# The two expert rows of a token are added into its residual row by the gathering DMA itself

## The chip, the cores and the metric

The kernel runs on one core of a Trainium2 chip. The metric is the device time of one execution in microseconds (us); before the change the median of three executions is 1997.67 us (1995.52 to 1998.90).

## The reference, cut to what matters

One layer of a hybrid encoder: a token mixer, an attention over a memory, and a hierarchical mixture of experts, each followed by a DeepNorm residual and a layer norm. The change touches the last of them alone. There are T = 1056 tokens of D = 1024 f32 values, and each token goes to two of 32 experts:

```
x = LN3(alpha * x + y[token, first expert] + y[token, second expert]),   alpha = 2 ** 0.25
LN: xc = x - mean(x);  xc * rsqrt(mean(xc * xc) + 1e-5) * g + b
```

The expert rows y already carry their gate factor.

## The kernel before

It is one program with an instruction stream for each engine, ordered by semaphores. SBUF is one large array, the arena, and its regions are reused from stage to stage. Tokens are handled in NT = 9 tiles of 128 rows (the ninth has 32). The residual rows after the second layer norm stay in SBUF as `x1` (nine tiles of 128x1024 f32) and are also stored to HBM, from where the experts' inputs are gathered.

**The expert loop** runs over 32 experts, then over spilled blocks (an expert takes at most C = 96 rows in its first block; two spilled blocks occur in this run). Per expert SP loads three weight matrices of 2 MB, PE multiplies in gate/up (L785) and down (L794) form, DVE turns blocks and finishes the silu (L1743 to L1756, in `dve_expert`), ACT scales the result by the gate and stores it to `y_blocks` in HBM (L1263, L1268). POOL gathers the inputs of an expert two ahead (L1938), as soon as DVE has turned the input block that used the buffer (L1756).

**The tail** starts when the last expert rows have landed in HBM; ACT then signals `fin_ready` (L1326). POOL issues 18 indirect DMAs (L1967), two for each tile: one into `g1` (the first expert's rows) and one into `g2` (the second's), both on the tile's semaphore `g_in[t]`. For six of the tiles (2, 4, 5, 6, 7, 8) POOL adds the pair itself (`pair_sum`, L1962), two tiles behind its gathers; for tiles 0, 1 and 3 DVE adds it (L1822). DVE then makes `alpha * x1 + g1` (L1825) and signals `sum_ready`. ACT takes the row sums with a copy pass (L1333), the negative mean (L1334, `mean_ready`), the squares (L1336) and the scale (L1337, L1338, `rstd_ready`). DVE centres the tile before (L1830), then scales the one before that (L1837), and SP stores each tile when DVE has scaled it (L880). The DVE loop is a software pipeline: in step s it sums tile s, centres tile s-1 and scales tile s-2, in this order, so the scaling of a tile always stands behind the centring of the next one.

Of the kernel before, what the change touches and what calls it, by code (L numbers as in the profile page):

```python
# [8 lines left out]
ALU = mybir.AluOpType  # L9
# [4 lines left out]
D = 1024  # L14
# [3 lines left out]
NT = (T + P - 1) // P  # L18
# [12 lines left out]
ALPHA = 2.0 ** 0.25  # L31
# [10 lines left out]
def rows_of(t):  # L42
    return P if t < NT - 1 else DEC


def cols_of(t):
    return slice(t * P, t * P + rows_of(t))


def build(nc, io):  # L50
    ctx = ExitStack()
    with ctx:
        def sem(name):
            return ctx.enter_context(nc.semaphore(name))
# [6 lines left out]
        def const(n):  # L61
            a = cpos[0]
            cpos[0] += n
            assert cpos[0] <= NCONST, cpos[0]
            return consts[:, a:a + n]
# [32 lines left out]
        dest_i = const(2 * NT).bitcast(U32).rearrange("p (k t) -> p k t", t=NT)  # L98
# [12 lines left out]
        def at(a, n):  # L111
            assert a + n <= ARENA, (a, n)
            return arena[:, a:a + n]

        def view(_at, names, **n):
            size = 1
            for v in n.values():
                size *= v
            return at(_at, size).rearrange(f"p ({names}) -> p {names}", **n)
# [41 lines left out]
        x1 = view(R, "t n", t=NT, n=D)  # L161
# [60 lines left out]
        place = route("k t n", k=2, t=NT, n=2 * NB)  # L222
        assert rt[0] <= R + 17408
        g1 = view(0, "t n", t=NT, n=D)
        g2 = view(NT * D, "t n", t=NT, n=D)
        scrap = at(R + 9216, D)
        PAIRS_DVE = (0, 1, 3)
        PAIRS_POOL = [t for t in range(NT) if t not in PAIRS_DVE]

        psum = ctx.enter_context(nc.psum_tensor("psum", [P, 8 * BANK], F32))  # L230

# [1 line left out]
        y_dram = nc.dram_tensor("y_blocks", [NB * C, D], F32, kind="Internal").ap()  # L233
# [34 lines left out]
        x2_stored = sem("x2_stored")  # L268
# [10 lines left out]
        o_xt, o_gu, o_h, o_dn, o_y = (sem(n) for n in ("o_xt", "o_gu", "o_h", "o_dn", "o_y"))  # L279
        o_gate = sem("o_gate")  # L280
        g_in = [sem(f"g_in{i}") for i in range(NT)]
        sum_ready, pair_ready = sem("sum_ready"), sem("pair_ready")
        fin_ready, mean_ready, centered = sem("fin_ready"), sem("mean_ready"), sem("centered")

        def banked(ps):
# [30 lines left out]
        def filled(eng, key):  # L316

            n, banks, _, _ = jobs[key]
            eng.wait_ge(pe_done, n)
            return psum[:, banks[0] * BANK:(banks[-1] + 1) * BANK]  # L320
# [6 lines left out]
        def emptied(eng, key):  # L327
            _, _, c, n = jobs[key]
            eng.wait_ge(evac[c], n + 1)
# [10 lines left out]
        def chain_of(eng, s):  # L340
            n = [0]

            def link(ins):
                n[0] += 1
                ins.then_inc(s, 1)
                eng.wait_ge(s, n[0])
            return link
# [49 lines left out]
        def score_cols(i):  # L397
            return (i + 1) * P if i < NT - 1 else PAST + DEC
# [661 lines left out]
        def _(act):  # L1060
            A = nc.scalar.activation
            link = chain_of(act, act_chain)
# [11 lines left out]
            for t in range(NT):  # L1074
                n = rows_of(t)
# [30 lines left out]
            for p, (tiles, nbuf, _, lag) in enumerate(FOX):  # L1106
                steps = [(i, h) for i in tiles for h in range(FH)]
                for s in range(len(steps) + lag + 3):
                    if s < len(steps):
                        i, h = steps[s]  # L1110
                        k = (FOX_FIRST[p] + s) // FH
# [5 lines left out]
                        nq, n = rows_of(i), score_cols(i)  # L1117
# [66 lines left out]
            for s in range(len(HG) + 2):  # L1184
                if s < len(HG):
                    n = rows_of(HG[s][1])
                    copy_job(("KE", s), keT[0:n, s % 3, :], filled(act, ("KE", s))[0:n, 0:P])
                if 0 <= s - 2 < len(HG):
                    h, c = HG[s - 2]
                    n = rows_of(c)  # L1190
# [37 lines left out]
            for s in range(NT + 3):  # L1228
                if s < NT:
                    n = rows_of(s)  # L1230
# [8 lines left out]
                if 1 <= s <= NT:  # L1239
                    u = s - 1  # L1240
                    n = rows_of(u)
# [4 lines left out]
                if s >= 3:  # L1246
                    u = s - 3
                    n = rows_of(u)
# [79 lines left out]
            for t in range(NT):  # L1328
                n = rows_of(t)
                y = x1[0:n, t, :]  # L1330
                total, neg_mean, squares, log_var, scale = (vals[0:n, i, t:t + 1] for i in range(5))
                act.wait_ge(sum_ready, t + 1)
                link(A(scrap[0:n, :], y, ACT.Copy, accum_out=total))  # L1333
                A(neg_mean, total, ACT.Copy, scale=-1.0 / D).then_inc(mean_ready, 1)  # L1334
                act.wait_ge(mean_ready, t + 1)
                link(A(scrap[0:n, :], y, ACT.Square, bias=neg_mean, accum_out=squares))  # L1336
                link(A(log_var, squares, ACT.Ln, bias=eps_ln[0:n, :], scale=1.0 / D))  # L1337
                A(scale, log_var, ACT.Exp, scale=-0.5).then_inc(rstd_ready, 1)  # L1338
# [3 lines left out]
        def _(dve):  # L1342
            V = nc.vector
            link = chain_of(dve, dve_chain)
            TS, TT, STT = V.tensor_scalar, V.tensor_tensor, V.scalar_tensor_tensor
# [4 lines left out]
            for t in range(NT):  # L1350
                n = rows_of(t)
# [41 lines left out]
            for p, (tiles, nbuf, _, lag) in enumerate(FOX):  # L1393
                steps = [(i, h) for i in tiles for h in range(FH)]
                for s in range(len(steps) + lag + 3):
                    if s < len(steps):
                        i, h = steps[s]
                        ps = filled(dve, ("S", p, s))
                        nq, n = rows_of(i), score_cols(i)
# [3 lines left out]
                    if (p, s) in FV_STEPS and FV_STEPS.index((p, s)) % 4 == 3:  # L1403
                        t = FV_LATE[FV_STEPS.index((p, s)) // 4]
                        n = rows_of(t)
# [13 lines left out]
                    if 0 <= u < len(steps) and u % FH == 0:  # L1419
                        i, k = tiles[u // FH], FOX_FIRST[p] // FH + u // FH  # L1420
# [14 lines left out]
            for m in range(HH):  # L1435
                k = hk[:, m, :]
# [4 lines left out]
            for m in range(HH):  # L1441
# [3 lines left out]
                for c in range(NT):  # L1445
                    b = hb[:, m, cols_of(c)]
# [44 lines left out]
            for t in range(NT):  # L1491
                n = rows_of(t)
# [10 lines left out]
            for s in range(len(HG) + 2):  # L1503
                if s < len(HG):
                    h, c = HG[s]
                    n = rows_of(c)
# [120 lines left out]
            for s in range(NT + 4):  # L1627
                if s < NT:
                    n = rows_of(s)
# [7 lines left out]
                if s >= 4:  # L1637
                    u = s - 4
                    n = rows_of(u)
# [8 lines left out]
                if 1 <= s <= NT:  # L1648
                    u = s - 1
                    n = rows_of(u)  # L1650
# [52 lines left out]
            for k, (E, GG) in enumerate(((E1, GA), (E2, GB))):  # L1703
                for t0, t1 in ((0, NT - 1), (NT - 1, NT)):
                    n, nt = rows_of(t0), t1 - t0
# [46 lines left out]
            def turn_h(b):  # L1752
                return V.transpose(hhT[:, b], hh.rearrange("p s (d k) -> p s k d", k=KE))  # L1753
# [4 lines left out]
            def x_turned(e, b, j):  # L1758
                dve.wait_ge(xe_in[b], 16 * NS * j + 16 * NS)
                if not isinstance(e, int) or e > 1:  # L1760
                    dve.wait_ge(gu_done, e - 1)
                turn_x(b).then_inc(xt_ready, 1)

            def dve_expert(e, b, j, last_one=False):

                if not last_one:
                    x_turned(e + 1, 1 - b, j + b)
                dve.wait_ge(g_exp, e + 1)
                silu_up(b, 4 * e)
                if not isinstance(e, int) or e > 1:  # L1770
                    dve.wait_ge(y_done, e - 1)
                turn_h(b).then_inc(h_ready, 1)
                if not isinstance(e, int) or e > 1:
                    dve.wait_ge(y_ready, e - 1)
                V.tensor_copy(gate2[:, b:b + 1, :], gates[:, bass.ds(e, 1), :]).then_inc(gate_ready, 1)

            x_turned(0, 0, 0)
            dve_expert(0, 0, 0)
            dve_expert(1, 1, 0)
            dve_expert(2, 0, 1)  # L1780
            with dve.Fori(1, NE // 2 - 1) as i:
                dve_expert(2 * i + 1, 1, i)
                dve_expert(2 * i + 2, 0, i + 1)
# [29 lines left out]


            dve.wait_ge(ln3_loaded, 32)
            for s in range(NT + 2):
                if s < NT:
                    n = rows_of(s)
                    y, g = x1[0:n, s, :], g1[0:n, s, :]
                    if s in PAIRS_DVE:  # L1820
                        dve.wait_ge(g_in[s], 32)
                        link(TT(g, g, g2[0:n, s, :], ALU.add))  # L1822
                    else:
                        dve.wait_ge(pair_ready, PAIRS_POOL.index(s) + 1)
                    STT(y, y, ALPHA, g, ALU.mult, ALU.add).then_inc(sum_ready, 1)  # L1825
                if 1 <= s <= NT:
                    t = s - 1
                    n = rows_of(t)
                    dve.wait_ge(mean_ready, t + 1)
                    STT(g1[0:n, t, :], x1[0:n, t, :], vals[0:n, 1, t:t + 1], ln3_par[0:n, 0, :], ALU.add, ALU.mult)\  # L1830
                        .then_inc(centered, 1)
                if s >= 2:
                    t = s - 2
                    n = rows_of(t)
                    dve.wait_ge(centered, t + 1)
                    dve.wait_ge(rstd_ready, 2 * NT + t + 1)
                    STT(x1[0:n, t, :], g1[0:n, t, :], vals[0:n, 4, t:t + 1], ln3_par[0:n, 1, :], ALU.mult, ALU.add)\  # L1837
                        .then_inc(ln_ready, 1)
# [3 lines left out]
        def _(pool):  # L1842
            Q = nc.gpsimd
            link = chain_of(pool, pool_chain)
# [79 lines left out]
            for t in range(NT):  # L1924
                n = rows_of(t)
# [30 lines left out]
                    gather(NE + j, j % 2, o_x[j % 2])  # L1956

            pool.wait_ge(fin_ready, 1)
            def pair_sum(t):
                n = rows_of(t)  # L1960
                pool.wait_ge(g_in[t], 32)
                Q.tensor_tensor(g1[0:n, t, :], g1[0:n, t, :], g2[0:n, t, :], ALU.add).then_inc(pair_ready, 1)  # L1962

            for t in range(NT):
                n = rows_of(t)
                for k, g in enumerate((g1, g2)):
                    pool.indirect_dma_start(out=g[0:n, t, :], out_offset=None, in_=y_dram,  # L1967
                                            in_offset=bass.IndirectOffsetOnAxis(ap=dest_i[0:n, k, t:t + 1], axis=0))\
                        .then_inc(g_in[t], 16)
                if t - 2 in PAIRS_POOL:  # L1970
                    pair_sum(t - 2)
            for t in range(NT - 2, NT):
                if t in PAIRS_POOL:
                    pair_sum(t)

# [28 lines left out]
```

## Time and profile before

| | |
|---|---|
| median of three executions | 1997.67 us |
| the profiled execution, its own time | 1996.47 us |
| its span in the trace | 1994.1 us |
| busy: PE, DVE, ACT, POOL | 90%, 38%, 16%, 11% of the span |
| PE's last matmul ends | about 1929 us |
| `fin_ready` given (L1326) | 1935.2 us |
| first and last gather of the tail issued | 1935.4 and 1969.6 us |
| last store issued | 1991.7 us |

The span is the time from the first to the last record of the profiled execution. Its own time lies 2.4 us above the span and 1.2 us under the median. Times below are us from the start of the span unless said otherwise. The tail is the 59 us from 1935 to 1994.

### The profile page before, as it was taken

What the parts mean: (1) busy time and instruction counts of PE and PEld (TensorE: products, weight loads), DVE (VectorE), ACT (ScalarE), POOL (GpSimd) and SP (SyncE); (2) the same over time, 40 slices, a digit from 0 to 9 for tenths busy, and PEclk for the clock granted to TensorE, in tenths of its full rate; (3) what the DMA queues carried; (4) which work ended last, traced back from release to release, by engine and by line L of the source; (5) the groups of instructions that cost most, each with busy time, mean ns of one, the idle gap of its engine ahead of it and who ended that gap; (6) DMA issues with size and microseconds to landing.
All of it is one profiled execution on the core that took longest, in us unless ns stands there. A gap on an engine that the chain in (4) does not pass through costs nothing. (4 is left out here: it accounts for less than half of the span.)

```text
span 1994.1 us, 33667 instructions
## 1 busy us (share of the span) xinstructions
PE 1792.5 (90%) x14867; PEld 1131.6 (57%) x14867; DVE 750.0 (38%) x1089; ACT 309.1 (16%) x701; POOL 210.5 (11%) x196
## 2 busy tenths in 40 slices
PE   8999999999999779999998999939999999999650
PEld 4455568766654554445665665426666666666420
DVE  1111456534461653320012443364433333333227
ACT  1111223411010440111001111000101111111005
POOL 2100000000010420000000000032111111111016
PEclk9999999999999689999999999859999999999875
DMA  5341002001100203045111000349999999999826
GB/s 197 96 165 43 1 5 83 1 1 43 42 0 4 92 6 116 33 136 169 34 42 42 22 22 28 144 171 366 422 424 424 424 425 423 424 424 424 360 61 216
DMA packets 72862, 326.94 MB, mean 164 GB/s; under 512 B 13368, under 2 KB 27968, under 8 KB 59728
## 3 DMA queue, kind: packets, MB, share of 16 engines
q1 hardware_dynamic: 47840, 280.70, 35.1%
q10 hardware_dynamic: 17360, 22.03, 3.4%
q0 software_dynamic: 7584, 23.08, 3.2%
q8 instruction: 61, 1.00, 0.2%
q14 instruction: 17, 0.14, 0.0%
HBM read 288.05 MB, written 37.65 MB: 163 GB/s over the span
## 5 line engine op out<-in xcount | busy, mean ns | idle before, releaser
L785 PE MATMUL psum<-arena 128*32 128x256 f32 x6528 | 360.4, 380 | 32.0 <-issue 30.8
L418 PE MATMUL psum<-arena 128*128 128x352 f32 x1152 | 342.1, 460 | 0.0
L785 PEld LDWEIGHTS psum<-arena 128*32 128x32 f32 x6528 | 244.7, 110 | 146.5 <-issue 45.4
L427 PE MATMUL psum<-arena 128*128 128x512 f32 (+1 forms) x720 | 318.4, 601 | 5.9 <-DMA arena<-in_w_in 4.7
L418 PEld LDWEIGHTS psum<-arena 128*128 128x128 f32 x1152 | 219.3, 191 | 122.2 <-issue 1.1
L1348 DVE COPY arena<-psum 128x512 f32<-128x512 f32 (+7 forms) x135 | 90.9, 681 | 417.8 <-PE psum L427 221.6
L427 PEld LDWEIGHTS psum<-arena 128*128 128x128 f32 (+1 forms) x720 | 131.7, 185 | 177.4 <-issue 175.5
L794 PE MATMUL psum<-arena 128*32 128x256 f32 x3264 | 189.7, 389 | 24.1 <-DVE arena L1753 24.1
L794 PEld LDWEIGHTS psum<-arena 128*32 128x32 f32 x3264 | 125.4, 113 | 82.0 <-DVE arena L1753 25.5
L1743 DVE TENSOR_SCALAR arena<-arena 128x384 f32<-128x384 f32 x34 | 12.2, 360 | 357.1 <-ACT arena L1284 315.3
L1065 ACT ACTIVATE arena<-psum 128x128 f32<-128x128 f32 (+5 forms) x181 | 86.5, 495 | 349.8 <-PE psum L411 276.2
L1938 POOL DMA_INDIRECT arena<-x_rows,consts x102 | 96.7, 948 | 414.1 <-DVE arena L1756 386.0
L411 PE MATMUL psum<-consts,arena 128*128 128x128 f32 (+4 forms) x819 | 121.8, 280 | 12.4 <-ACT arena L1065 6.3
L411 PEld LDWEIGHTS psum<-consts,arena 128*128 128x128 f32 (+4 forms) x819 | 97.2, 154 | 59.0 <-issue 30.8
L643 PE MATMUL psum<-arena 128*128 128x512 f32 (+1 forms) x288 | 125.3, 593 | 0.0
L1545 DVE SCALAR_TENSOR_TENSOR arena<-arena,psum 128x1024 f32<-128x1024 f32 (+1 forms) x18 | 22.0, 1220 | 185.8 <-PE psum L427 103.8
L1263 ACT ACTIVATE arena<-psum,consts 128x256 f32<-128x256 f32 x102 | 40.9, 471 | 324.0 <-DMA y_blocks<-arena 270.6
L643 PEld LDWEIGHTS psum<-arena 128*128 128x128 f32 (+1 forms) x288 | 51.5, 181 | 68.3 <-issue 67.9
L1745 DVE RECIPROCAL arena<-arena 128x384 f32<-128x384 f32 x34 | 86.8, 2553 | 1.2
L546 PE MATMUL psum<-arena 128*128 128x64 f32 (+2 forms) x624 | 76.5, 266 | 0.0
L511 PE MATMUL psum<-arena 66*128 66x512 f32 (+3 forms) x192 | 75.6, 502 | 0.5 <-DVE consts L1348 0.5
L1118 ACT ACTIVATE arena<-psum,consts 128x128 f32<-128x128 f32 (+8 forms) x72 | 51.3, 713 | 150.5 <-DVE consts L1401 148.7
(243 smaller groups left out, 1402.1 us busy)
## 6 DMA issues: line engine op xcount, KB each, us to landing
arena<-in_moe_w_down SPq DMA_DIRECT2D x34, 2048.0 KB, 22.6
arena<-in_moe_w_gate SPq DMA_DIRECT2D x34, 2048.0 KB, 16.9
arena<-in_moe_w_up SPq DMA_DIRECT2D x34, 2048.0 KB, 22.0
arena<-in_w_in SPq DMA_DIRECT2D x7, 2048.0 KB, 9.8
y_blocks<-arena ACTq DMA_DIRECT2D x136, 96.0 KB, 2.0
y_blocks<-arena ACTq DMA_DIRECT2D x1, 8448.0 KB, 44.0
arena<-in_x_prompt SPq DMA_DIRECT2D x9, 512.0 KB, 3.3
arena<-in_w_out SPq DMA_DIRECT2D x2, 2048.0 KB, 11.0
```

What stands on the lines that cost most here:

```text
L411: return nc.tensor.transpose(out, a, ident[0:n, 0:n])
L418: last = mm(ps[0:m, c * BANK:c * BANK + THIRD], lhs(k), rhs[:, k, c * THIRD:(c + 1) * THIRD], start=(k == 0), stop=(k == KD - 1))
L427: last = mm(ps[0:n, c * 512:(c + 1) * 512], lhs(k), rhs(k, c), start=(k == 0), stop=(k == KD - 1))
L511: last = mm(ps[0:nq, c:e], q, ka[0:KX, h, c:e], start=True, stop=True)
L546: last = mm(ps_o[0:nq, h * FD:(h + 1) * FD], probsT[p][0:w_, u % nbuf, b, 0:nq], v, start=(b == 0), stop=(b == len(blocks) - 1))
L643: last = mm(psum[0:n, b:b + BANK], mixT[:, k, cols_of(t)], wrows[:, k, c * 512:(c + 1) * 512], start=(k == 4), stop=(k == 3))
L785: last = mm(out, xeT[:, b, a, k, :], gu[b][:, :, k, j * P:(j + 1) * P], start=(k == 0), stop=(k == KD - 1))
L794: last = mm(B_Y[b][32 * j:32 * j + 32, a * 256:(a + 1) * 256], hhT[:, b, a, k, :], wd[b][:, k, j * 256:(j + 1) * 256], start=(k == 0), sto ...
L1065: take(A(out, src, ACT.Copy), key)
L1348: take(V.tensor_copy(out, src), key)
L1745: V.reciprocal(sg, sg).then_inc(silu_step, 1)
L1938: pool.indirect_dma_start(out=xe[:, b, a, :], out_offset=None, in_=x2_quarters, in_offset=bass.IndirectOffsetOnAxis(ap=tok_idx[:, e, a:a + ...
```

## The change

- The gathers of the tail write `x1` itself with an addition: the DMA adds each gathered row to what stands in SBUF. `g2`, `pair_sum`, DVE's pair sums and DVE's `alpha * x1 + g1` go.
- Two additions into one tile may not be in flight together, so POOL first issues the first rows' gather of tile s, and then waits for the landing of tile s-3's before it issues the second rows' gather of that tile (`GATHER_LAG = 3`).
- `x1` must hold `alpha * x1` before. DVE does this in the expert loop: three tiles each behind experts 0, 1 and 2, once the rows are stored to HBM. POOL waits for all nine (`x2_scaled`).
- ACT's row sums and DVE's centring wait for the gathers' semaphore (32, both landed) where they had waited for DVE or POOL.

```
-            dve_expert(0, 0, 0)
-            dve_expert(1, 1, 0)
-            dve_expert(2, 0, 1)
+            dve.wait_ge(x2_stored, 16 * NT)
+            for e, b, j in ((0, 0, 0), (1, 1, 0), (2, 0, 1)):
+                dve_expert(e, b, j)
+                for t in range(3 * e, 3 * e + 3):
+                    y = x1[0:rows_of(t), t, :]
+                    TS(y, y, ALPHA, None, ALU.mult).then_inc(x2_scaled, 1)
...
-            for s in range(NT + 2):
-                if s < NT:
-                    n = rows_of(s)
-                    y, g = x1[0:n, s, :], g1[0:n, s, :]
-                    if s in PAIRS_DVE:
-                        dve.wait_ge(g_in[s], 32)
-                        link(TT(g, g, g2[0:n, s, :], ALU.add))
-                    else:
-                        dve.wait_ge(pair_ready, PAIRS_POOL.index(s) + 1)
-                    STT(y, y, ALPHA, g, ALU.mult, ALU.add).then_inc(sum_ready, 1)
-                if 1 <= s <= NT:
+            for s in range(1, NT + 2):
+                if s <= NT:
                     t = s - 1
                     n = rows_of(t)
+                    dve.wait_ge(g_in[t], 32)
                     dve.wait_ge(mean_ready, t + 1)
...
-            def pair_sum(t):
-                n = rows_of(t)
-                pool.wait_ge(g_in[t], 32)
-                Q.tensor_tensor(g1[0:n, t, :], g1[0:n, t, :], g2[0:n, t, :], ALU.add).then_inc(pair_ready, 1)
...
+            def add_rows(k, t):
+                n = rows_of(t)
+                pool.indirect_dma_start(out=x1[0:n, t, :], out_offset=None, in_=y_dram,
+                                        in_offset=bass.IndirectOffsetOnAxis(ap=dest_i[0:n, k, t:t + 1], axis=0),
+                                        compute_op=ALU.add).then_inc(g_in[t], 16)
+
+            pool.wait_ge(x2_scaled, NT)
+            for s in range(NT + GATHER_LAG):
+                if s < NT:
+                    add_rows(0, s)
+                if s >= GATHER_LAG:
+                    pool.wait_ge(g_in[s - GATHER_LAG], 16)
+                    add_rows(1, s - GATHER_LAG)
```

## Rows read from the trace of the kernel before

**Rows 1.** The page: busy time of each engine.

```profile
PE 1792.5 (90%) x14867; PEld 1131.6 (57%) x14867; DVE 750.0 (38%) x1089; ACT 309.1 (16%) x701; POOL 210.5 (11%) x196
```

**Rows 2.** Chain that ended last, in order of time (start, us, what).

```profile
1934.95 0.21 ACT consts L1326
...
1935.42 0.94 POOL arena L1967
...
1970.53 2.65 POOL arena L1962
```

**Rows 3.** Groups by line, 1935 to 1995 (busy us, mean ns, idle before).

```profile
L1967 POOL DMA_INDIRECT arena<-y_blocks,consts x18 | 22.6, 1256 | 102.6 <-ACT consts L1326 97.8 <-issue 4.7
L1962 POOL TENSOR_TENSOR arena<-arena 128x1024 f32<-128x1024 f32 (+1 forms) x6 | 15.9, 2668 | 0.1
L1830 DVE SCALAR_TENSOR_TENSOR arena<-arena 128x1024 f32<-128x1024 f32 (+1 forms) x9 | 13.6, 1508 | 0.0
L1837 DVE SCALAR_TENSOR_TENSOR arena<-arena 128x1024 f32<-128x1024 f32 (+1 forms) x9 | 13.5, 1505 | 0.0
L1825 DVE SCALAR_TENSOR_TENSOR arena<-arena 128x1024 f32<-128x1024 f32 (+1 forms) x9 | 13.1, 1456 | 6.8 <-POOL arena L1962 6.7
...
L1822 DVE TENSOR_TENSOR arena<-arena 128x1024 f32<-128x1024 f32 x3 | 3.7, 1221 | 21.2 <-DMA arena<-y_blocks,consts 21.2
```

**Rows 4.** Timeline of the tail (start, duration, engine, line).

```profile
1944.34 1.06 ACT L1333 ACTIVATE arena<-arena 128x1024 f32<-128x1024 f32 x1 [9.18 <-DVE arena L1825]
...
1945.52 0.20 ACT L1334 ACTIVATE arena<-arena 128x1 f32<-128x1 f32 x1
...
1947.70 1.06 ACT L1333 ACTIVATE arena<-arena 128x1024 f32<-128x1024 f32 x1
...
1969.64 0.88 POOL L1967 DMA_INDIRECT arena<-y_blocks,consts  x1 [0.30 <-issue]
...
1976.47 3.38 DVE L1830 SCALAR_TENSOR_TENSOR arena<-arena 128x1024 f32<-128x1024 f32 x1
...
1989.22 2.46 DVE L1837 SCALAR_TENSOR_TENSOR arena<-arena 128x1024 f32<-128x1024 f32 x2
1991.71 0.33 SPq L880 DMA_DIRECT2D out_y_s<-arena  x1
```

**Rows 5.** DMA, 1936 to 1976: queues (packets, MB, share), issues (median us to landing).

```profile
q0 software_dynamic: 2400, 8.65, 64.7%
q1 hardware_dynamic: 576, 2.10, 13.1%
...
out_y_p<-arena SPq DMA_DIRECT2D x4, 512.0 KB, 4.3
arena<-y_blocks,consts POOLq DMA_INDIRECT x18, 6.1
```

**Rows 6.** Windows; the last two columns are DMA busy share and GB/s.

```profile
1936.00:1941.00 5.00, 0.00 (x0) 0.00 (x0) 0.00 (x0) 0.00 (x0) 3.78 (x5) 0.50 0.75 240
...
1946.00:1951.00 5.00, 0.00 (x0) 0.00 (x0) 2.83 (x3) 4.58 (x11) 4.67 (x3) 0.50 0.98 383
```

**Rows 7.** DMA, 1400 to 1800, the queue of the weight loads.

```profile
q1 hardware_dynamic: 10365, 150.97, 88.7%
```

**Rows 8.** Timeline between experts 0 and 1.

```profile
1356.93 0.13 DVE L1775 COPY consts<-arena 128x3 f32<-128x3 f32 x1
1356.96 1.60 DVE L1756 STREAM_TRANSPOSE arena<-arena 128x768 f32<-128x768 f32 x1
1358.84 0.95 POOL L1938 DMA_INDIRECT arena<-x_rows,consts  x1 [10.54 <-DVE arena L1756]
...
1362.30 0.36 DVE L1743 TENSOR_SCALAR arena<-arena 128x384 f32<-128x384 f32 x1 [3.73 <-ACT arena L1284]
```

**Rows 9.** Groups by line and shape, DVE: multiplications by a scalar, slowest and typical.

```profile
L1467 DVE TENSOR_SCALAR arena<-arena 128x1056 f32<-128x1056 f32 x4 | 7.2, 1798 | 0.0
...
L1444 DVE TENSOR_SCALAR arena<-arena 128x1056 f32<-128x1056 f32 x4 | 2.8, 700 | 0.0
```

More of the change, by code:

```diff
@@ L224, in build @@
         g1 = view(0, "t n", t=NT, n=D)
-        g2 = view(NT * D, "t n", t=NT, n=D)
         scrap = at(R + 9216, D)
-        PAIRS_DVE = (0, 1, 3)
-        PAIRS_POOL = [t for t in range(NT) if t not in PAIRS_DVE]
+        GATHER_LAG = 3
         psum = ctx.enter_context(nc.psum_tensor("psum", [P, 8 * BANK], F32))
@@ L281, in build @@
         g_in = [sem(f"g_in{i}") for i in range(NT)]
-        sum_ready, pair_ready = sem("sum_ready"), sem("pair_ready")
+        x2_scaled = sem("x2_scaled")
         fin_ready, mean_ready, centered = sem("fin_ready"), sem("mean_ready"), sem("centered")
@@ L1331, in _ @@
                 total, neg_mean, squares, log_var, scale = (vals[0:n, i, t:t + 1] for i in range(5))
-                act.wait_ge(sum_ready, t + 1)
+                act.wait_ge(g_in[t], 32)
                 link(A(scrap[0:n, :], y, ACT.Copy, accum_out=total))
@@ L1958, in _ @@
             pool.wait_ge(fin_ready, 1)
-            def pair_sum(t):
+            def add_rows(k, t):
                 n = rows_of(t)
-                pool.wait_ge(g_in[t], 32)
-                Q.tensor_tensor(g1[0:n, t, :], g1[0:n, t, :], g2[0:n, t, :], ALU.add).then_inc(pair_ready, 1)
-            for t in range(NT):
-                n = rows_of(t)
[L1966 to L1974, printed above, removed]
+                pool.indirect_dma_start(out=x1[0:n, t, :], out_offset=None, in_=y_dram,
[8 more added lines that the diff above has]
+                    add_rows(1, s - GATHER_LAG)
 _INS = ["x_prompt", "x_sample", "cache_fox_k", "cache_fox_v", "cache_fox_logf", "state_hgrn", "cache_mem_k",
```

## The prediction, made before the changed kernel was run

> **What bounds the kernel now.** First the busy times [rows 1]: PE is busy for 90% of the span, so nothing that only spares DVE or POOL work beside the matmuls can show. The change pays, if at all, where PE has stopped. The chain that ended last, in order of time, says where that is [rows 2]: after ACT's signal at 1935.0 to 1935.2 the end hangs on POOL, which issues gathers and adds pairs from 1935.4 to 1973.2, and then on DVE. The groups by line of that tail [rows 3] give POOL's work: 22.6 us of gather issues and 15.9 us of pair sums, 38.5 us almost without a break. DVE has 13.1 + 13.6 + 13.5 + 3.7 = 43.9 us in 59. The reader should see two things: POOL sets the pace of the first two thirds, since no sum can start before its pair; and the two disturb each other, since DVE's centring takes 1.27 us alone and 3.38 beside POOL's additions [rows 4]. The DMA queues [rows 5] show what is not yet the bound: in 40 us the gathers take 64.7% of the 16 engines and the stores 13.1%. The windows [rows 6] say how near it is: once several gathers are in flight the engines are 98% busy at 383 GB/s.
>
> **What the edits remove.** Six pair sums (15.9 us) leave POOL, nine STT and three TT (16.8 us) leave DVE [rows 3], and with them their disturbance. POOL is left with 18 issues of 0.94 us and a gap of 0.30 us, 1.25 us apart (first issue and mean, [rows 2, 3]): 22.5 us, done by 1958 if nothing blocks it.
>
> **What they add in the expert loop.** Nine multiplications of a 128x1024 tile by a number. The nearest rows have 1056 columns: 0.70 us, and 1.80 in the mean of a group that runs beside POOL's work [rows 9]. I take 0.7: three make 2.1 us behind each of experts 0 to 2. The wait for `x2_stored` in front is met, since the first turned input was gathered from those stored rows. What stands behind the first group is DVE's turning of input 2 (1356.96, 1.60 us), then the silu of expert 1, which starts at 1362.30 after 3.73 us without work [rows 8]. So 2.1 us are covered, and POOL's next gather, released by that turning, starts 2.1 us later for an expert that is not due for another round. At 1.8 us each, 5.4 us would stand against 3.7 of cover: 1.7 us late once. Price 0, with 0 to 2 us for the range.
>
> **What the tail becomes.** Three paths, of which the slowest ends it.
>
> (a) ACT. From one row sum to the next it takes 1947.70 - 1944.34 = 3.36 us [rows 4], as soon as both rows of a tile have landed. The second gather of tile 0 is the fifth issue, at 1935.4 + 4 x 1.25 = 1940.4; a landing takes 6.1 us from the issue [rows 5], so 1946.5. Eight tiles more: 1973.4 for the last row sum's start. Behind it: 1.4 us to the negative mean (1944.34 to 1945.72, [rows 4]), 0.1 for the signal, three DVE operations at 1.2, 1.2 and 1.27 (two scalings in 2.46 [rows 4]), and 2.4 us from DVE's last result (1991.68) to the end of the span for the last store: 7.6 in all. End 1981.0.
>
> (b) The DMA engines. The price of an adding gather stands in no row. What stands is: a gathered row of 4 KB takes 0.647 x 40 x 16 / 2112 = 0.196 us of one engine [rows 5]; 4 KB of the streamed weights takes 0.887 x 400 x 16 / 150.97 x 0.004096 = 0.154 us [rows 7], so a gathered row has 0.042 us of its own; a stored tile takes 0.131 x 40 / 4 = 1.3 us of all engines [rows 5]. Let p be an engine's time for an added row. The engines start late: 25% of the first 5 us are lost [rows 6], so they count from 1937.3. Before tile 7 is complete they do 2080 rows (2080 p / 16 = 130 p) and six stores (7.9 us). Then tile 7 takes 3.4 us on ACT until tile 8, of 32 rows and landed by then, follows, and 7.6 as above. End = 1937.3 + 7.9 + 11.0 + 130 p = 1956.2 + 130 p.
>
> (c) POOL, 22.5 us and its waits. It waits for the landing of the gather issued some five issues before. Three or more others are always queued behind that one, so the engines do not run dry and the wait is inside (b).
>
> For p the two ends: 0.196, the addition costs the engines nothing, gives 1981.7 (-12.4, so (a) and (b) then almost meet). Two whole packets, 0.392, give 2007.2 (+13.1). An adding row must read both the row in HBM and the one in SBUF. Two streamed reads, 0.309, give 1996.4 (+2.3). I take two streamed reads and once the 0.042 us that a gathered row has over a streamed one: 0.351, end 2001.8, which is +7.7. Between ends this far apart this is the row that it is nearest to: the same gather, with one more plain 4 KB moved. No change comes out at p = (1994.1 - 1956.2) / 130 = 0.292, half as dear again as now. That is the number on which everything hangs.
>
> The Trainium skill, Collectives: The Full Stack, "The bandwidth ceiling: the fold count and why AG ≠ RS ≠ AR", speaks against the change: a reducing transfer is not slow for its addition, but because it puts two reads on the read ring of its engine, and so runs at half the rate. It gives about 31 GB/s for an engine, hence as an estimate 0.264 us for 4 KB with two reads, an end of 1990.5 and a gain of 3.6. No row here shows an adding DMA; 26.6 GB/s (4096 B in 0.154 us) is what an engine moves in this trace.
>
> Sum: the profiled execution's 1996.47 + 7.7 = 2004.2. Against the median of 1997.67 the same change would be 2005.4; I give 2004. The 2.4 us around the span are taken as unchanged.
>
> **The rivals.** What a measurement of this kernel can tell from no change is about 0.2%, 4 us.
>
> - *The addition is hidden (p up to 0.22).* The engines already hold several packets at once, and the read in SBUF may lie under the longer one in HBM; for it, the busy share of 0.98 at 383 GB/s shows that the time of a packet is not all movement. Against: the same share says there are no idle engines to hide in. End 1981.7 to 1985, -12.4 to -9: 1984 to 1987 as a time. This is the case on the other side, and it decides below p = 0.26, where the gain passes 4 us. A partial hiding, p 0.22 to 0.28, gives 1987 to 1995.
> - *The two reads count, and nothing else.* The gathered row's extra is waiting that the second read covers: p 0.28 to 0.32, 1995 to 2000, around 1998.8. The rule of the Collectives page would be this one. It is no measurable change.
> - *The DMA does them one after the other.* Each added row costs a read, a read and a write that do not overlap: three times 0.196 = 0.59 us, end 2032.7, a time of 2035 (+38). For it speaks only that an addition needs both operands at hand before it writes; from p = 0.45, a time of 2017, this case holds.
> - *POOL becomes the bound.* Issuing an adding gather takes it longer, since each row needs one more descriptor. At 2.5 us for 1.25, the second gather of tile 7, the last but one, goes out 16 x 2.5 = 40 us after the first, at 1975.4, lands 6.1 us later, and 11.0 behind it give 1992.5: -1.6, no measurable change. Against: a gather of 32 rows costs it hardly less than one of 128 (0.88 us for the last issue [rows 4] against 0.94 for the first [rows 2]), so the number of descriptors is not what it waits for.
>
> **How the numbers follow.** Two reads and the row's own extra (p 0.32 to 0.45, around 2004): 0.38. Hidden: 0.18. Partly hidden: 0.08. Two reads alone: 0.17. One after the other: 0.13. POOL: 0.06. Faster by over 4 us: 0.18 + 0.07 = 0.25. Within 4 us (1993.7 to 2001.7): 0.01 of the partly hidden, 0.15 of the two reads, 0.05 of POOL and 0.03 of the forecast's low end, 0.24. Slower: the rest, 0.51. The range, 1984 to 2018, reaches from the hidden case, whose lower edge it cuts off, to where the serial one begins, with the expert loop's 0 to 2 us inside it, and leaves out some 0.17. Cases of both signs hold much of the chance; the likeliest one's own range is 1999 to 2017.
>
> **What would show it.** In the queue's row for the stretch from 1936 on: q0's share times the stretch times 16 over 2112 is p; 0.35 confirms the step, 0.2 or 0.6 does not. Its bytes tell whether both reads are counted. The windows should show the engines at 0.95 or more until tile 7 has landed, near 1990, and ACT's idle time before L1333 put down to the gathers' DMA; with the first pair landing about 1951, 16 us of it lie between the first tile and tile 7 (1990.8 - 1951.3 - 7 x 3.36). DVE's centring and scaling should all take 1.27 us. POOL's issues should stay near 0.95 us, its idle time now waits for landings. The nine multiplications should take 0.7 us each and PE should reach its last matmul at 1929, as before. The prediction is wrong if p is, or if landing an adding gather takes so much longer than its transfer that POOL's waits let the queue run empty.

## The result, and the profile after

Twenty executions of each kernel give 2002.2 us after the change against 1998.92 us before, a ratio of 1.0017 with a 95% interval of 1.001 to 1.0024: 3.3 us slower, 2.0 to 4.8 by the interval. It is a real loss, and a little under the 4 us that the prediction called distinguishable.

The profiled execution after the change has a span of 2001.7 us. Its expert loop starts 4.3 us later than that of before (DVE turns the first input at 1341.96 in place of 1337.65), ahead of any edited instruction. So the two spans must not be subtracted; what can be compared is the tail, from the end of ACT's signal to the end of the span. Before it is 1994.1 - 1935.16 = 58.9 us [rows 2], after it is 2001.7 - 1939.93 = 61.8 us: 2.9 us longer, which agrees with the medians. All tails below are measured in this way.

The timeline of the tail after the change (start, duration, engine, line; L1324 is the signal, L1954 the gathers, L1331 the row sums, L1823 the centring):

```profile
1939.72 0.20 ACT L1324 ACTIVATE consts<-consts 128x1 f32<-128x1 f32 x1
1940.19 1.61 POOL L1954 DMA_INDIRECT arena<-y_blocks,consts  x1 [97.68 <-ACT consts L1324]
...
1957.79 1.06 ACT L1331 ACTIVATE arena<-arena 128x1024 f32<-128x1024 f32 x1 [17.86 <-DMA arena<-y_blocks,consts]
...
1979.92 1.06 ACT L1331 ACTIVATE arena<-arena 128x1024 f32<-128x1024 f32 x1 [3.35 <-DMA arena<-y_blocks,consts]
...
1981.41 1.29 DVE L1823 SCALAR_TENSOR_TENSOR arena<-arena 128x1024 f32<-128x1024 f32 x1 [4.08 <-ACT arena L1332]
...
1990.79 1.06 ACT L1331 ACTIVATE arena<-arena 128x1024 f32<-128x1024 f32 x1
...
1999.07 0.33 SPq L878 DMA_DIRECT2D out_y_s<-arena  x1
```

The reader should see three things. The first row sum starts 17.9 us after the signal; before it was 9.2 [rows 4]. ACT then waits for a DMA in front of five more tiles, 28.5 us in all, of which 17.9 are this start. And DVE's centring takes 1.28 us everywhere: the disturbance by POOL's additions [rows 4] is gone, and the tail is longer all the same.

Who waited for whom in the tail (us in total, times, longest), and then the gathers themselves (shortest, median and longest issue in ns, and the time from issue to landing):

```profile
ACT arena L1331 <- DMA arena<-y_blocks,consts: 28.5, 6, 17.9
POOL arena L1954 <- DMA arena<-y_blocks,consts: 9.9, 3, 4.8
```

```profile
L1954 POOL DMA_INDIRECT arena<-y_blocks,consts x18: 1355/1541/2320, 1940.2 to 1981.6; - x18
DMA to landing us min/median/max: 6.2/12.3/18.5
```

A gather now lands 12.3 us after its issue in the median, where it was 6.1 [rows 5]: the gathers stand queued in front of the engines.

The windows, to be held against [rows 6] (the last two columns are the engines' busy share and GB/s):

```profile
1941.00:1946.00 5.00, 0.00 (x0) 0.00 (x0) 0.00 (x0) 0.00 (x0) 4.09 (x4) 0.50 0.74 122
1946.00:1951.00 5.00, 0.00 (x0) 0.00 (x0) 0.00 (x0) 0.00 (x0) 4.39 (x3) 0.50 1.02 193
1951.00:1956.00 5.00, 0.00 (x0) 0.00 (x0) 0.00 (x0) 0.00 (x0) 4.09 (x4) 0.50 1.06 206
...
1966.00:1971.00 5.00, 0.00 (x0) 0.00 (x0) 2.51 (x3) 3.09 (x7) 2.71 (x2) 0.50 1.06 210
...
1986.00:1991.00 5.00, 0.00 (x0) 0.00 (x0) 4.31 (x4) 4.81 (x12) 0.00 (x0) 0.50 1.02 285
```

The engines are full from 1946 to 1991 and, while only gathers run, move 193 and then 206 to 210 GB/s. Next come the gathers' queue over the whole tail, from 1936 to 1996, the same queue while nothing else moves, from 1951 to 1966, and the stores that move from 1960 until tile 7 has landed at 1990.76:

```profile
q0 software_dynamic: 2400, 8.65, 74.4%
```

```profile
q0 software_dynamic: 854, 3.12, 106.0%
```

```profile
q1 hardware_dynamic: 627, 2.32, 20.0%
```

The bytes are those written: 8.65 MB as before [rows 5]. If the engines read every byte of `x1` as well, the profile does not count it, and it shows in the time alone. 3.12 MB in 15 us on 16 engines is 208 GB/s, or 4096 x 16 / 208e3 = 0.315 us of an engine for an added row. The prediction's own measure, the queue's share, gives more: 0.744 x 60 x 16 / 2112 = 0.338 over the tail, and 0.334 in the full stretch. The share there is 106%, more than the engines have, so the times of packets overlap; divided by 1.06 the 0.334 is the 0.315 again. What follows uses the 0.315.

In the expert loop the hoisted multiplications (L1781) lie where they were expected; compare [rows 8]:

```profile
1361.27 1.89 DVE L1781 TENSOR_SCALAR arena<-arena 128x1024 f32<-128x1024 f32 x3
1363.07 1.61 DVE L1754 STREAM_TRANSPOSE arena<-arena 128x768 f32<-128x768 f32 x1
1366.60 0.36 DVE L1741 TENSOR_SCALAR arena<-arena 128x384 f32<-128x384 f32 x1 [1.93 <-ACT arena L1282]
```

Three take 1.89 us, and DVE still has 1.93 us without work before the silu. PE's last matmul ends at 1933.5 where it ended at 1929.1: 4.4 us later, of which 4.3 stood there before the first edited instruction.

### The profile page after: what moved, and what is told of

Read it like the earlier page. It is cut to its first block and busy times, and to the rows that moved or that the text cites. A ratio compares the mean times of both kernels' runs of the same rounds, so it can differ in the third digit from the quotient of the medians.

```text
span 2001.7 us, 33668 instructions
## 1 busy us (share of the span) xinstructions
PE 1794.1 (90%) x14867; PEld 1132.6 (57%) x14867; DVE 735.4 (37%) x1086; ACT 309.2 (15%) x701; POOL 201.5 (10%) x190
## 5 line engine op out<-in xcount | busy, mean ns | idle before, releaser
L641 PEld LDWEIGHTS psum<-arena 128*128 128x128 f32 (+1 forms) x288 | 51.5, 181 | 68.3 <-issue 67.9
```

Of the source, the lines that this page charges most:

```text
L641: last = mm(psum[0:n, b:b + BANK], mixT[:, k, cols_of(t)], wrows[:, k, c * 512:(c + 1) * 512], start=(k == 4), stop=(k == 3))
```

## The experiments

**e1: the addition alone taken away.** The gathers overwrite `x1`; order and waits stay. This leaves out the sum of the expert rows and the residual.

```
-                                        in_offset=bass.IndirectOffsetOnAxis(ap=dest_i[0:n, k, t:t + 1], axis=0),
-                                        compute_op=ALU.add).then_inc(g_in[t], 16)
+                                        in_offset=bass.IndirectOffsetOnAxis(ap=dest_i[0:n, k, t:t + 1], axis=0)).then_inc(g_in[t], 16)
```

> The changed kernel with its gathers overwriting x1 in place of adding to it; this leaves out the sum of the two expert rows and the residual, everything else (order, waits, sizes, ACT's and DVE's work) stays. Theory (the addition's second read on the DMA engines): a row falls from 0.31 to 0.20 us of an engine, POOL's issue from 1.54 to 0.94 us, and the tail (from ACT's signal to the end) from 61.8 to 46-47 us, where ACT's 3.4 us a tile and the DMA meet; time about 15 us under the change, ratio to before 0.994. Rival (POOL's order and its waits for landings are what costs): the waits are still there, so the tail stays above 55 us.

Measured: 1983.51 us, ratio to before 0.9937 (0.9922 to 0.9952); tail 1981.0 - 1936.59 = 44.4 us. The gathers' queue from 1948 to 1952, when nothing else moves, then the waits of the tail:

```profile
q0 software_dynamic: 452, 1.64, 102.1%
```

```profile
ACT arena L1331 <- DMA arena<-y_blocks,consts: 11.7, 1, 11.7
POOL arena L1954 <- issue: 5.2, 17, 0.3
```

1.64 MB in 4 us are 411 GB/s, 0.160 us a row. The one missing word doubles the rate (411 / 208 = 1.98) and takes 17.4 us out of the tail. ACT waits once, for the first tile, and then runs through; POOL waits for no landing although the waits are still in its program. So with plain gathers order and waits cost nothing; whether they cost something with adding gathers is the question of e5. The edit also shortens POOL's issues from 1.54 to 0.94 us, but these were not the price: after the change the gathers already stood queued, up to 18.5 us before they landed. The 17.4 us are not all that the engines save, for ACT is now the bound. The tail ends 1.6 us under the lower of the expected 46 and 47: an ACT that finds its tile landed goes from one row sum to the next in 3.1 to 3.2 us (after the change, 1987.64 to 1990.79), where 3.36 was taken.

**e2: half of each row.** Both gathers add 512 of 1024 columns; the other half of the expert rows is left out.

```
-                pool.indirect_dma_start(out=x1[0:n, t, :], out_offset=None, in_=y_dram,
+                pool.indirect_dma_start(out=x1[0:n, t, 0:512], out_offset=None, in_=y_dram,
```

> The changed kernel with both gathers adding only the first 512 of a row's 1024 columns; the other half of the expert rows is left out. Same number of gathers, rows and waits, half the bytes. Theory (two reads, each by its bytes): a row of 2 KB takes 0.15-0.16 us of an engine and the tail falls to 47-50 us, ACT's floor. Rival (a fixed cost of each added row in the DMA's adder or in the wait for its operands): a row stays above 0.25 us and the tail above 57 us. Rival (POOL's longer issues and its waits): issues stay at 1.54 us, and the tail stays above 55 us.

Measured in a single execution of 1992.84 us: tail 1990.7 - 1939.62 = 51.1 us, between the expectations. The windows of e2, and its POOL group:

```profile
1946.00:1951.00 5.00, 0.00 (x0) 0.00 (x0) 0.00 (x0) 0.00 (x0) 4.13 (x3) 0.50 0.93 135
1951.00:1956.00 5.00, 0.00 (x0) 0.00 (x0) 1.29 (x1) 2.87 (x6) 4.35 (x3) 0.50 0.94 140
```

```profile
L1954 POOL DMA_INDIRECT arena<-y_blocks,consts x18 | 30.5, 1694 | 105.8 <-ACT consts L1324 100.6 <-issue 5.2
```

The issues are as long as for whole rows (1.69 us in the mean), with 0.3 between them 2.0 us apart, and POOL waits for no landing. Its 36 us of issues now set the pace, up to tile 4; behind that ACT runs at its own 3.1 us a tile and ends the tail. The 18 gathers come no faster than POOL gives them out, so the 140 GB/s are no rate of the engines, and e2 gives only an upper limit: 2 KB cost an engine at most 2048 x 16 / 140e3 = 0.23 us, against 0.315 for 4 KB. The removed half of the bytes was worth at least 0.08 us a row. That a row has no fixed share at all is not shown; that the bytes, and not only the number of rows, set the price is. No run separates a second read from an addition that runs at half the rate: either could double the time of each byte.

**e3: one of the two gathers adds.** The first adds into `x1`, the second goes plainly into `g1`, and DVE adds it. No order between them is needed.

```
+                    dve.wait_ge(g_in[s], 32)
+                    TT(y, y, g1[0:n, s, :], ALU.add).then_inc(sum_ready, 1)
...
+                for k, out in enumerate((x1, g1)):
+                    how = {"compute_op": ALU.add} if k == 0 else {}
+                    pool.indirect_dma_start(out=out[0:n, t, :], out_offset=None, in_=y_dram,
```

> Half of the change: the first gather of a tile adds into x1, the second goes plainly into g1 and DVE adds g1 to x1 (one tensor-tensor a tile); the two gathers need no order, so the lag and its waits are gone; no pair sums on POOL, scaling in the expert loop. Theory (DMA reads): rows at 0.31 and 0.20 us alternate, 130 x 0.255 = 33 us, tail 2.1 + 7.9 + 33 + 12.4 = 55.6 us, against 58.9 before and 61.8 after: time 3 us under before, ratio 0.998. Rival (the change costs through order and waits, not through reads): tail 50-52 us, ratio 0.996. Rival (DVE's three operations a tile bind): 9 x 3.7 = 33 us behind the first tile at 12, with 6 behind: 51 us.

Measured: 1992.51 against 1997.23 us, ratio 0.9985 (0.9966 to 1.0004); tail 1991.3 - 1937.53 = 53.8 us. The waits and two windows of e3:

```profile
DVE arena L1822 <- DMA arena<-y_blocks,consts: 32.5, 6, 22.4
```

```profile
1954.00:1959.00 5.00, 0.00 (x0) 0.00 (x0) 4.54 (x4) 4.09 (x11) 4.23 (x3) 0.50 1.06 265
...
1969.00:1974.00 5.00, 0.00 (x0) 0.00 (x0) 3.59 (x4) 3.09 (x7) 0.00 (x0) 0.50 1.05 315
```

With half the adding gathers the tail falls by 8.0 of the 17.4 us that all of them are worth, and DVE waits for DMAs to the last full tile. The sum by reads said 55.6 with 0.196 us for a plain row; with the 0.160 of e1 it is 2.1 + 7.9 + 130 x 0.2375 + 12.4 = 53.3. By the interval the time is not proven under that of before. But the interval is widened by a single execution of 2012.37 us; the other ten, 1991.38 to 1995.62, all lie under the fastest of before (1995.77), and the tails are 5.1 us apart.

**e4: the multiplications alone moved**, in the kernel before.

```
+                for t in range(3 * e, 3 * e + 3):
+                    y = x1[0:rows_of(t), t, :]
+                    TS(y, y, ALPHA, None, ALU.mult)
...
-                    STT(y, y, ALPHA, g, ALU.mult, ALU.add).then_inc(sum_ready, 1)
+                    TT(y, y, g, ALU.add).then_inc(sum_ready, 1)
```

> The kernel before with the nine multiplications by alpha moved into the expert loop as in the change, and DVE's alpha * x1 + g1 in the tail replaced by x1 + g1. Theory: the multiplications (0.7 us each) are covered by DVE's idle time in the expert loop, the tail is as before (58.9 us), ratio 0.999 to 1.001. Rival (the hoisted work delays the expert loop or its gathers): experts end 2 us or more later, ratio 1.001 and up.

Measured: 1997.36 against 1997.23 us, ratio 1.0003 (0.9994 to 1.0012); tail 1999.1 - 1940.28 = 58.8 us. The hoisting costs nothing and brings nothing, and a second trace gives the tail of before to 0.1 us.

**e5 and e6: the lag.** `GATHER_LAG` 6 and 1 in place of 3.

> The changed kernel with GATHER_LAG = 6 in place of 3: the second gather of a tile goes out behind the first gather of the tile six further on, so POOL finds its landing long done. Theory (the engines' time for 18 adding gathers is the bound, whatever their order): POOL's 9.9 us of waits for landings shrink, the engines stay at a share of 1.0 or more and 205-210 GB/s, ACT's first tile comes 6 to 8 us later, tail 59 to 62 us (61.8 at 3). Rival (the order and POOL's waits cost the time): tail 52 to 56 us.

> The changed kernel with GATHER_LAG = 1: the second gather of a tile waits for the first one's landing with one other gather behind it. Theory (engines bound): the first pair lands about 12 us after ACT's signal in place of 17.9, the tail stays within 61 to 64 us; POOL waits more and nothing else changes, as long as some gather is always queued. Rival (landing latency): the queue runs dry between gathers, the engines' share falls under 0.9 and the tail grows beyond 66 us.

Measured: tails of 1998.7 - 1935.19 = 63.5 us (lag 6) and 2005.5 - 1938.11 = 67.4 us (lag 1), both above the range of my theory, the second in that of its rival. Waits and windows of the kernel with lag 6:

```profile
POOL arena L1954 <- DMA arena<-y_blocks,consts: 1.8, 1, 1.8
```

```profile
1946.00:1966.00 20.00, 0.00 (x0) 0.00 (x0) 1.28 (x1) 3.09 (x7) 16.65 (x12) 0.50 1.06 203
```

and with lag 1:

```profile
POOL arena L1954 <- DMA arena<-y_blocks,consts: 20.4, 8, 3.2
```

```profile
1946.00:1951.00 5.00, 0.00 (x0) 0.00 (x0) 0.00 (x0) 0.00 (x0) 4.09 (x4) 0.50 0.90 147
...
1981.00:1986.00 5.00, 0.00 (x0) 0.00 (x0) 2.48 (x2) 3.09 (x7) 2.27 (x2) 0.50 1.06 260
...
1991.00:1996.00 5.00, 0.00 (x0) 0.00 (x0) 1.28 (x3) 1.92 (x6) 0.00 (x0) 0.50 0.59 168
```

With lag 6 POOL is freed of 8 of its 9.9 us of waits, and the tail gains nothing: the engines are as full as at lag 3 (1.06) and do 203 GB/s. That is the theory's point, and it holds: the rival in which the waits are the price falls here. What it missed are the ends. With lag 1 the engines are not full near the start (0.90 and 147 GB/s from 1946 to 1951): 25 us after the signal they have moved 4.08 MB of gathered rows, where it is 4.48 MB at lag 3, about 2 us of work at 208 GB/s. Nor are they full at the end. The last full tile's second gather waits for the first and goes out only at 1985.09, 47.0 us after the signal (36.8 at lag 3); it lands at 1994.5, with the engines at 0.59 in the last stretch, 5.6 us later after the signal than the 50.8 of lag 3. With lag 6 that landing is at 52.6 us. Of these 1.7 us, 1.0 would be the rate, as an estimate (8.5 MB at 203 in place of 208 GB/s); why the rate is lower was not settled. Each is a single execution (2000.80 and 2007.64 us).

**e7: a mix made from these prices.** As e3, but in tiles 1, 4 and 6 no gather adds and DVE adds both.

```
+        PLAIN = (1, 4, 6)
...
+                    if s in PLAIN:
+                        link(TT(y, y, g2[0:n, s, :], ALU.add))
                     TT(y, y, g1[0:n, s, :], ALU.add).then_inc(sum_ready, 1)
...
+                for k, out in enumerate((g2 if t in PLAIN else x1, g1)):
+                    how = {"compute_op": ALU.add} if out is x1 else {}
```

> As e3_one_add, but in tiles 1, 4 and 6 neither gather adds; DVE adds both (two tensor-tensor operations). Theory (a plain row takes 0.16 us of an engine in a full queue, an adding one 0.31): three adding gathers turned plain spare 3 x 128 x 0.154 / 16 = 3.7 us of the engines, three more operations cost DVE 3.7 us where it had about 7 us without work; tail 50 to 51.5 us against 53.8 in e3_one_add and 58.9 before, ratio to before 0.996. Rival (DVE is the bound in e3_one_add already): tail 55 us or more.

Measured: 1988.25 against 1998.23 us, ratio 0.9949 (0.9936 to 0.9963); tail 1991.5 - 1942.60 = 48.9 us, 10 us shorter than before and a little under the expected 50 to 51.5. It beats both kernels. Two windows of it:

```profile
1964.00:1969.00 5.00, 0.00 (x0) 0.00 (x0) 4.97 (x6) 3.27 (x9) 4.32 (x3) 0.50 1.02 352
1969.00:1974.00 5.00, 0.00 (x0) 0.00 (x0) 5.00 (x5) 4.50 (x11) 1.59 (x1) 0.50 1.05 335
```

DVE (the third pair of columns, 4.97 and 5.00 of 5 us) and the DMA engines are now full together; the work is balanced, and DVE is where it ends.

## Why the prediction was right, and in which term it was not

**The place and the bound.** Right: the bound moved from POOL to the DMA engines, which are full until tile 7 has landed. e1 shows that the addition is the cause (-17.4 us of tail without it), e3 that taking away half of it gives about half back (8.0), and e5 that POOL's waits are not.

**The sum's form.** It said: end of tail = 2.1 us after the signal + 7.9 for six stores + 130 p + 11.0. With the measured p = 0.315 this is 62.0 us against 61.8. Tile 7 starts at 1990.79 on ACT, 50.9 after the signal; by the sum 51.0. That it is so close is in part luck, since two terms are off in opposite directions. The engines start late by 3.5 us, not 2.1: from the signal to 1951, in 11.1 us, they move 1.57 MB of gathered rows, 7.6 us of work at 208 GB/s. And only 2.32 MB of stores, 4.4 tiles, move before tile 7 lands, 5.8 us in place of 7.9. The short last tile's rows are through by then too, so the engines have done 2112 rows: 3.5 + 5.8 + 132 x 0.315 = 50.9.

**The mis-sized term is p.** "I take two streamed reads and once the 0.042 us that a gathered row has over a streamed one: 0.351" is the step that was off. By the test that the prediction set itself, the share of q0, p is 0.338 and would confirm it; but that share runs over 100%, and what sets the time is the 0.315 of an engine. The 0.042 is not there in a full queue: e1 moves gathered rows at 0.160 us, nearly the weights' 0.154 [rows 7]. The 0.196 us of [rows 5] is a mean over 40 us of which only some were full, and [rows 6] already had the better number: 383 GB/s on 0.98 of 16 engines are 0.168 us a row. What made the packets take longer in the other stretches, waiting or the stores beside them, was not taken apart. An added row is 0.315, twice the 0.160, so p was 0.036 too high; 130 times that is 4.7 us, nearly all that lies between forecast and trace, and the forecast's +7.7 became +2.9 in the tail and +3.3 in the medians. What came true, by its p of 0.28 to 0.32, is the rival "the two reads count, and nothing else", to which I had given 0.17 and 1998.8 us (+2.3). That the second half of the price is a read, and not the addition itself, is argued and not shown. Part of why 2004.0 looks close to 2002.2 is chance: the twenty executions of before lie 1.3 us above the three on which the prediction stood, and the profiled one 2.4 us below them.

The Trainium skill, Collectives: The Full Stack, "The bandwidth ceiling: the fold count and why AG ≠ RS ≠ AR", had the ratio: half the rate for two reads. The runs agree, with 208 against 411 GB/s. Its 31 GB/s for an engine is not reached here: 411 / 16 = 25.7 with one read.

**POOL.** The rival of longer issues was half right: an adding gather is issued in 1.54 us in place of 0.94, so 1.84 apart. With whole rows it stays hidden behind the engines' 2.5 us a gather (128 x 0.315 / 16); in e2 it set the pace up to tile 4. That the number of rows does not matter to POOL was no argument against it.

**The expert loop.** Price 0, as said: 0.63 us a multiplication (0.7 was taken), 1.9 us of cover left, ratio 1.0003 in e4.

**ACT's waits.** 28.5 - 17.9 = 10.6 us after the first tile in place of 16, since the engines were faster than said and the first pair came 1.8 us later. From tile 5 on ACT runs at its own pace (row sums at 1984.48, 1987.64, 1990.79), which the sum did not foresee. It came out right by coincidence: tile 7's second gather, issued at 1976.76, lands 14.0 us later, at 1990.76, just when ACT arrives.

**(c), the waits inside (b).** Right at lag 3. As a general statement it is too strong: in e6 the engines are at 0.90 near the start and 0.59 at the end.

## What to carry to other kernels

Before an addition is moved into a DMA, ask whether the DMA engines have the time for it: here it costs what a second plain transfer of the same bytes would, and pays only as far as the engines were idle. Split such work over the engines until they are full together, as in e7, rather than moving all of it. And price a transfer from a stretch in which its queue is full; a share of busy time divided by rows can contain waiting, and where it passes 100% it counts the same time twice.

## What the runs showed of the hardware that was not expected

An indirect DMA with an addition takes POOL 1.54 us to issue, against 0.94 without (128 rows each), and as long for rows of 2 KB as of 4 KB. Gathered rows of 4 KB run nearly at the pace of the streamed weights as soon as several gathers are queued: 411 GB/s in e1, against 424 in the page's slices of the expert loop before. In e3 the plain gathers of full tiles were issued in 0.96 to 1.00 us up to 1950 and in 1.55 to 1.62 us from 1952 on, although they do not add. Plain issues of 1.3 to 2.0 us among others of 0.94 stand in e1 and in the kernel before as well; why was not looked into.
